# The 512 columns of the feed-forward up projections, read in alternating runs of the high and the low half

## The reference: two transformer blocks, 256 tokens, width 2048

```python
def first_block(x, ...):                      # x: (1, 256, 2048), all float32
    z = rms_norm(h, attn_norm_g) @ w_in       # 2048 x 5120
    ...                                       # differential attention, gated spatial mixing
    h = h + mixed @ w_out
    f = rms_norm(h, ffn_norm_g)
    h = h + (silu(f @ ffn_w1) * (f @ ffn_w3)) @ ffn_w2     # 2048 -> 5632 -> 2048
    h = h + (p @ pl_w_up) * sigmoid(h @ pl_w_gate)

def second_block(x, ...):                     # 16 meta tokens + 256 tokens
    ...                                       # pooling and convolution branches, gates
    gate, up = split(rms_norm_2(h, norm_ffn_g) @ w_gate_up)
    h = h + (silu(gate) * up) @ w_down        # 2048 -> 5632 -> 2048
```

## Time and profile before

| | |
|---|---|
| median of 3 runs | 2670.3 us (2670.2 to 2670.61) |
| profiled execution: span from first to last instruction | 2668.2 us |
| PE busy, share of the span | 2657.2 us, 100% |
| PEld busy | 2349.5 us, 88% |
| DVE busy | 1658.2 us, 62% |
| ACT busy | 1235.8 us, 46% |
| HBM traffic | 188 GB/s over the span |

### The profile page before, as it was taken

One profiled execution on the slowest core, in us unless ns is written; L12 is line 12 of the kernel. 1 busy time (PEld: TensorE's weight loads), 2 busy tenths in 40 slices (PEclk: granted clock), 3 DMA queues, 4 the chain that ended last, 5 costly groups with the idle time before them and its releaser, 6 DMA issues.

```text
span 2668.2 us, 39872 instructions
## 1 busy us (share of the span) xinstructions
PE 2657.2 (100%) x15711; PEld 2349.5 (88%) x15711; DVE 1658.2 (62%) x1645; ACT 1235.8 (46%) x1355; POOL 0.8 (0%) x7
## 2 busy tenths in 40 slices
PE   9999999999999999999999999999999999999998
PEld 7889888888888888888999999888888888888887
DVE  6567766555655556796676666556765645564555
ACT  5446554444444444565443333444554434443444
POOL 0000000000000000000000000000000000000000
PEclk9999999999999999999999999999999999999999
DMA  8554555556555555555555555555565555555554
GB/s 291 183 174 144 192 187 189 191 189 191 192 191 191 191 191 188 175 197 198 176 183 178 179 184 190 189 189 189 189 205 189 189 190 189 189 195 195 178 190 140
DMA packets 254251, 502.92 MB, mean 188 GB/s; under 512 B 8130, under 2 KB 11652, under 8 KB 253988
## 3 DMA queue, kind: packets, MB, share of 16 engines
q1 hardware_dynamic: 252180, 497.61, 56.5%
q10 hardware_dynamic: 1952, 3.68, 0.4%
HBM read 498.37 MB, written 2.88 MB: 188 GB/s over the span
## 4 chain that ended last, share of the span: by engine, by line
PE 99%; DVE 0%; ACT 0%; DMA 0%; issue 0%; ACTq 0%; DVEq 0%
PE ps L1356 49%; PE ps L1370 24%; PE ps L1389 4%; PE ps L1390 4%; PE ps L1391 4%; PE ps L1407 4%; PE ps L1408 4%; PE ps L1409 4%; PE ps L1399 0%; PE ps L1401 0%; PE ps L1400 0%; PE ps L1319 0%; DMA xtok<-in_x_dram 0%; PE ps L1543 0%; PE ps L1542 0%; PE ps L1544 0%
## 5 line engine op out<-in xcount | busy, mean ns | idle before, releaser
L822 DVE TENSOR_TENSOR lo<-raw,hi 128x1024 fp32r<-128x1024 f32 x940 | 1127.6, 1223 | 856.5 <-ACT hi L488 847.6
L488 ACT ACTIVATE hi<-raw 128x1024 fp32r<-128x1024 f32 x940 | 971.3, 1055 | 1065.3 <-PE ps L1370 479.0
L1356 PE MATMUL ps<-A,hi 128*128 128x512 f32 x3648 | 859.9, 392 | 0.0
L1356 PEld LDWEIGHTS ps<-A,hi 128*128 128x128 f32 x3648 | 675.1, 188 | 138.9
L1356 PE MATMUL ps<-B,hi 128*128 128x512 f32 x1984 | 481.7, 395 | 0.0
L1370 PEld LDWEIGHTS ps<-A,lo 128*128 128x128 f32 x3648 | 442.6, 188 | 11.5 <-DVE lo L822 0.2
L1370 PE MATMUL ps<-A,lo 128*128 128x256 f32 x3648 | 445.4, 278 | 0.0
L1356 PEld LDWEIGHTS ps<-B,hi 128*128 128x128 f32 x1984 | 364.4, 188 | 79.3
L1370 PEld LDWEIGHTS ps<-B,lo 128*128 128x128 f32 x1984 | 243.0, 188 | 10.3
L1370 PE MATMUL ps<-B,lo 128*128 128x256 f32 x1984 | 244.5, 277 | 0.0
L1408 PE MATMUL ps<-B,hi 128*128 128x258 f32 (+1 forms) x768 | 219.8, 286 | 0.0
(11 more groups left out here) (240 smaller groups left out, 1341.1 us busy)
## 6 DMA issues: line engine op xcount, KB each, us to landing
raw<-in_w_in_dram SPq DMA_DIRECT2D x136, 1024.0 KB, 5.1
raw<-in_ffn_w_dram SPq DMA_DIRECT2D x132, 1024.0 KB, 5.1
raw<-in_w_gate_up_dram SPq DMA_DIRECT2D x88, 1024.0 KB, 5.0
raw<-in_w_down_dram SPq DMA_DIRECT2D x44, 1024.0 KB, 5.1
raw<-in_w_out_dram SPq DMA_DIRECT2D x16, 1024.0 KB, 5.1
raw<-in_pl_w_gate_dram SPq DMA_DIRECT2D x16, 1024.0 KB, 5.1
raw<-in_conv_out_w_dram SPq DMA_DIRECT2D x16, 1024.0 KB, 5.1
raw<-in_w_o_dram SPq DMA_DIRECT2D x16, 1024.0 KB, 5.1
```

Source lines behind the costliest of these rows:

```text
L488: act.activation(hi[:, slot % RING], raw[:, raw_slot, 2 * (slot % 2):2 * (slot % 2) + 2, :], ACT.Copy).then_inc(hi_ready, 1)
L822: dve.tensor_tensor(lo[:, slot % RING], raw[:, slot // 2 % RAWS, 2 * (slot % 2):2 * (slot % 2) + 2, :], hi[:, slot % RING], ALU.subtract). ...
L1356: last = pe.matmul(ps[:, b0 + m, :], high(slot, kk, m), both, start=j == 0 and kk == 0, stop=ends and j == seg.pieces - 1 and kk == 1)
```

## The change

The table names the six up segments and gives each a run length: 16 columns in the first network and 4 in the last. In `highs` the moving operand and the PSUM output of these segments are then walked in another order: e high columns, the e low columns of the same tokens, the next e high ones, and so on. Output and input are walked alike, so each column still lands where it did. `lows`, the other segments and every other engine's code are as they were; the number and the order of the instructions do not change.

```diff
+IN_TURNS = {f"f{i}_up{c}": e for i, e in ((1, 16), (2, 4)) for c in range(3)}
 SNAKED = {"qk", "out"} | {f"f{i}_{part}{c}" for i in (1, 2) for part in ("up", "down") for c in range(3)}
...
                 X = activations(buf, layout)
                 pe.wait_ge(hi_ready, n + 1)
+                e = IN_TURNS.get(seg.name)
                 for kk in range(2):
                     k = 2 * j + kk + (4 * WIDEST_FIRST[g] if seg.name == "pool" else 0)
                     for m in range(MT):
                         both = X[:, k, 0:2 * T] if layout == "halves" else X[:, k, META:META + 2 * T]
-                        last = pe.matmul(ps[:, b0 + m, :], high(slot, kk, m), both, start=j == 0 and kk == 0,
+                        to = ps[:, b0 + m, :]
+                        if e:
+                            both, to = (x.rearrange("p (h c e) -> p c h e", h=2, e=e) for x in (both, to))
+                        last = pe.matmul(to, high(slot, kk, m), both, start=j == 0 and kk == 0,
                                          stop=ends and j == seg.pieces - 1 and kk == 1)
```

## The result

The changed kernel takes 2721.97 us (2721.72 to 2722.06, 4 runs) against 2670.25 (2670.16 to 2670.61, 4 runs) before: ratio 1.0194, 95% interval 1.0181 to 1.0206. It is 51.7 us slower; 21.7 us faster was forecast, and 2722 lies above the range (2630 to 2683). The profiled execution has a span of 2719.7 us, 51.5 more than before.

A forecast was written before the change was run, and what follows sets the result against it. PE was taken as the bound, busy throughout. From the profiled span of 2668.2 us, 21.7 us came off for high matmuls, other terms 0: span 2646.5, time 2648.6 us; range 2630 to 2683.

The forecast's parts named there:

- What bounds the kernel: Whole kernel: PE is busy throughout at the top clock, so time is the sum of the paces of 15711 matmuls.
- Distance modulo 256 bytes: Plain high matmuls: where the moving operand begins relative to the stationary one sets the pace, 228.75 or 233.1 ns.
- two walks that meet: In SBUF: the moving stream and next weights' load get in each other's way, a guess for the extra 15.4 ns.
- they will come differently: 2816 high matmuls of the ups: the new walk changes the meetings, halving the extra; 7.7 ns each, 21.7 us saved.
- the bad end of this mechanism: High matmuls of the ups: at worst the slower pace the trace knows, 233.1 ns, +12.2 us.
- Breaks cost 0: High matmuls of the ups: 222,000 breaks between runs taken as free; upper end +178 us.
- The row of ScalarE: ScalarE's write: 16 runs of 16 elements take 419 ns, as one run of 256 does, so a break costs 0.
- Rival 3: Inside the 2816 high matmuls: each break takes time in PE's reader or PSUM accumulation; 2763 or 2848 us; chance 0.13.
- Low matmuls: 2816 low matmuls of the ups: their two paces, 113.1 and 118.1 ns, may shift by 7.0 us either way; taken 0.
- Rival 4: High matmuls of the ups: the new relation of walks is worse, 233.1 ns; 2676.4 or 2682.5 us; chance 0.13.
- Supply: Up stretches: ScalarE's and VectorE's splits and the DMAs still keep ahead of a faster PE; cost 0.
- The rule of two read ports: PE: loading the next weights takes no SBUF bandwidth from the running matmul, so the change would give nothing.

## Why the prediction was wrong, step by step

- **What bounds the kernel: right.** Time is the sum of the paces, no wait took part, and every ns of pace counted: 1408 x 11.1 ns + 1408 x 2.0 for the low ones = 18.4 us in the first network, and 512 x 22.8 + 512 x 20.6 + 384 x 23.2 = 31.1 plus 2.5 for the low ones = 33.6 in the last. Together 52.0, measured 51.5.
- **Distance modulo 256 bytes: right**, and shown by moving A and B. But it was given too much. The prediction laid all of the 15.4 ns over the bare columns to two walks that meet. The distance moves 4 to 5 ns of it. Some 5 ns remain even for one line over and over, and weights held at one place do not remove the rest: the plain read takes 232.2 ns with them.
- **The step that failed** is this one: "they will come differently", and half of the extra goes, "because a low run and its high run at one place leave the rest of the places free to the other stream twice as long". The term of the sum was 2816 matmuls at -7.7 ns; measured are +11.1 ns each in the first network and +20.6 to +23.2 in the last. The moving read's own return to a place was left out. With e = 4 each line is followed at once by one at the same place: 64 returns x 0.53 = 34 ns over the 218.6 of one line, 252.5 ns; measured 249.5 to 252.6. With e = 16 none returns at once, but a place comes again after 4 lines and not after 16: 240.0. That this return is what costs is shown by the run with the same 31 breaks and the places in plain order (228.91); its size is measured and not derived. The sign was chosen on an argument about the other stream, and the bad end of this mechanism, 233.1 ns, was taken from rows in which the walk was plain, so it was no bound on a walk of another kind.
- **Breaks cost 0: right**, now shown with 31 and 127 of them. The row of ScalarE gave the right value and that of VectorE not, with some luck: neither is of PE, and breaks that do not keep the places in order are not free. Rival 3, the only one that put the time as high, had the right place in part (the reader inside the 2816 matmuls) and the wrong cause. Its rule from "PSUM — Partial Sum Buffer" of the Trainium skill, in the table of specifications, that any non-contiguous pattern slows matmuls, is not seen: on the output alone, runs of 4 and 16 columns took 228.9 ns as a plain one does.
- **Low matmuls:** 0 was taken with +7.0 us as the bad bound; they went to the slower pace nearly throughout, +5.3 us.
- **Rival 4** named the slower relation of the walks, with 233.1 ns. The direction was right, but its 6.1 to 12.2 us are an eighth to a quarter of the 51.7, and the distance was not the cause: the walked reads are the same at every distance tried.
- **Supply: right.** PE waited for no split, before or after.
- **The rule of two read ports** ("TensorE: Matmul & The Clock Gate" of the Trainium skill, in the section on what happens when a matmul is issued) was set against the mechanism. The runs go against the rule in part (the operands' distance moves a plain matmul by 4 to 5 ns, weights with step 0 or 2 by 3 to 4), and against the prediction in the rest: some 47 of the 52 us are in the high matmuls, whose price is the moving read's alone.

Open: the price of a return after 2 or more lines. All that was run lies between 233 and 244 ns, falls towards 229 at 16 lines, and is not a function of that count alone (e = 16 with jumps of 256, 512 and 1024 bytes returns after 4 lines each time and takes 233.4, 236.4 and 240.0). Nor do the runs show where the 10 ns between one line over and over and a plain read come from: a plain read has no return at once and would be at 218.6 by the rule of 0.53 ns, so that rule fits the walks that return at once and no others. Open too is why f2_up1 is at 249.5 and f2_up2 at 252.2 with the same e = 4.

## What to carry over

For the moving operand of a `float32r` matmul of 512 columns, the one kind tried, it is not contiguity that counts but the order of 16-byte lines modulo 256 bytes: strides are free as long as lines are read whole and the places come in turn, and going on to a new line a multiple of 256 bytes away is the dearest of the reads by whole lines (286.9 ns). Where PE is busy throughout, the start addresses of the moving and the stationary operand relative to each other are worth a look: moving a small buffer ahead of a large one, with a second offset in its rows for the last network, gave 7 us of 2670 here. And a segment-by-segment table of paces lets one run carry six variants, if the trace repeats a plain segment to a tenth of a nanosecond and each variant is held against its own segment.

## What was not expected of the hardware

- A matmul of 512 `float32r` columns took from 217.9 to 482.9 ns by the pattern of its moving read alone, at a granted clock of 1.00.
- Two columns of a 16-byte line at a time: 453 ns with lines in order, 483 when each next pair lay 264 bytes on; 327 with e = 2 on the walk of the change.
- Two lines read in turns, even at one place and 1024 bytes apart, are as cheap as one (218.3 ns); four lines over and over are not (241.2).
- The distance of moving and stationary operand modulo 256 bytes moves a plain 512-column matmul between 228.0 and 233.7 ns and a 256-column one between 113.9 and 119.7, and the two do not have their best at the same distance.
- A weight load that takes every fourth column (16 bytes from one to the next) shows 313 ns, against 188 for columns side by side and 195 for every second one.
